# A layer boundary in quarters, a reordered attention tail and an attention without filler products, in a one-core fp32 transformer kernel

## The reference

```python
for i in range(2):                                   # first block
    h = h + 0.5 * rmsnorm(swiglu(rmsnorm(h)))        # sublayers 0 and 3
    m = neighborhood_attention(...) if i == 0 else diff_attention(...)   # 1 and 4
    h = h + rmsnorm(m)
    h = h + 0.5 * rmsnorm(swiglu(rmsnorm(h)))        # 2 and 5
x = h[:, 16:]                                        # second block
x = x + rms_norm(concat(moba_attention(...), mlstm(...)) @ w_out)        # 6
x = x + rms_norm(square(relu(rms_norm(x) @ w_up)) @ w_down)              # 7
```

## Time and profile before

| | |
|---|---|
| time before, median of 3 runs | 1430.26 us (1430.21 to 1435.5) |
| the profiled execution | 1431.02 us, span 1429.2 us |
| PE, PEld busy | 99%, 95% of the span |
| DVE, ACT, POOL busy | 67%, 46%, 3% |
| granted TensorE clock | 1.00 |
| chain that ended last | PE 92%, DVE 4%, ACT 2% |

### The profile page before, as it was taken

The page is one execution under the profiler, slowest core; times in us unless marked ns, Lnnn a source line. Parts: engine busy times, 40 slices in busy tenths (PEclk is TensorE's granted clock), DMA queues, the critical chain, the costliest instruction groups (busy, mean ns, idle before and its releaser), DMA issues.

```text
span 1429.2 us, 26250 instructions
## 1 busy us (share of the span) xinstructions
PE 1415.9 (99%) x10980; PEld 1358.7 (95%) x10980; DVE 950.5 (67%) x1242; ACT 663.5 (46%) x891; POOL 45.0 (3%) x72
## 2 busy tenths in 40 slices
PE   9999999999999999999999999999999999999998
PEld 9999999978999999999999988999999997999887
DVE  6666568565966556866556678776556875787653
ACT  5444436454544334544435357554344455544432
POOL 0000010010000001000001000000001010000000
PEclk9999999999999999999999999999999999999999
DMA  6586765511455576455455640465556540356552
GB/s 220 179 227 189 207 186 172 177 62 53 154 177 176 170 206 211 154 177 177 139 174 159 206 148 2 153 201 185 186 181 200 178 148 31 119 180 212 183 196 98
DMA packets 238911, 234.11 MB, mean 164 GB/s; under 512 B 29791, under 2 KB 233492, under 8 KB 238816
## 3 DMA queue, kind: packets, MB, share of 16 engines
q1 hardware_dynamic: 238024, 232.33, 52.2%
q10 hardware_dynamic: 792, 0.40, 0.1%
HBM read 231.52 MB, written 1.12 MB: 163 GB/s over the span
## 4 chain that ended last, share of the span: by engine, by line
PE 92%; DVE 4%; ACT 2%; issue 1%; DMA 1%; DVEq 0%; SPq 0%; ACTq 0%
PE acc L649 22%; PE acc L648 22%; PE acc L650 22%; PE acc L718 3%; PE aux L888 2%; PE aux L887 2%; PE aux L886 2%; PE acc L724 2%; PE aux L948 1%; PE aux L649 1%; PE aux L650 1%; PE aux L648 1%; PE acc L1161 1%; PE acc L1269 1%; PE aux L1180 1%
## 5 line engine op out<-in xcount | busy, mean ns | idle before, releaser
L648 PE MATMUL acc<-x_hi,w_hi 128*128 128x272 f32 (+1 forms) x1960 | 559.6, 286 | 0.8 <-DVE x_lo L2239 0.6
L649 PE MATMUL acc<-x_lo,w_hi 128*128 128x272 f32 (+1 forms) x1960 | 559.7, 286 | 0.0
L650 PE MATMUL acc<-x_hi,w_lo 128*128 128x272 f32 (+1 forms) x1960 | 557.9, 285 | 0.0
L1880 DVE TENSOR_TENSOR w_lo<-raw,w_hi 128x2048 fp32r<-128x2048 f32 (+2 forms) x224 | 470.3, 2104 | 107.1 <-ACT w_hi L1407 106.7
L1407 ACT ACTIVATE w_hi<-raw 128x2048 fp32r<-128x2048 f32 (+3 forms) x246 | 397.5, 1621 | 156.6 <-DMA raw<-in_ffn_w_down 48.0
L648 PEld LDWEIGHTS acc<-x_hi,w_hi 128*128 128x128 f32 x1960 | 369.4, 188 | 3.6 <-issue 1.7
L649 PEld LDWEIGHTS acc<-x_lo,w_hi 128*128 128x128 f32 x1960 | 368.2, 188 | 0.3 <-issue 0.2
L650 PEld LDWEIGHTS acc<-x_hi,w_lo 128*128 128x128 f32 x1960 | 368.4, 188 | 0.0
L648 PE MATMUL acc<-hid_hi,w_hi 128*128 128x272 f32 (+1 forms) x704 | 201.9, 287 | 0.0
L649 PE MATMUL acc<-hid_lo,w_hi 128*128 128x272 f32 (+1 forms) x704 | 201.6, 286 | 0.0
L650 PE MATMUL acc<-hid_hi,w_lo 128*128 128x272 f32 (+1 forms) x704 | 200.7, 285 | 0.0
(11 more groups left out here) (340 smaller groups left out, 1668.0 us busy)
## 6 DMA issues: line engine op xcount, KB each, us to landing
raw<-in_ffn_w_gate SPq DMA_DIRECT2D x44, 1024.0 KB, 5.3
raw<-in_ffn_w_up SPq DMA_DIRECT2D x44, 1024.0 KB, 5.3
raw<-in_ffn_w_down SPq DMA_DIRECT2D x32, 768.0 KB, 4.5
raw<-in_ffn_w_down SPq DMA_DIRECT2D x32, 640.0 KB, 4.1
raw<-in_w_up SPq DMA_DIRECT2D x16, 1024.0 KB, 5.3
raw<-in_w_down SPq DMA_DIRECT2D x16, 1024.0 KB, 4.8
raw<-in_na_w_qkv SPq DMA_DIRECT2D x12, 1024.0 KB, 5.2
raw<-in_da_w_qkv SPq DMA_DIRECT2D x12, 1024.0 KB, 5.2
```

What stands on the lines that cost most here:

```text
L648: nc.tensor.matmul(o, wh, xh, start=first, stop=False)
L649: nc.tensor.matmul(o, wh, xl, start=False, stop=False)
L650: return nc.tensor.matmul(o, wl, xh, start=False, stop=last)
L1880: nc.vector.tensor_tensor(w_lo[:, slot, w], raw[:, slot, w], w_hi[:, slot, w].bitcast(F32), ALU.subtract)\
```

## The change

Four edits. The panel after the second mixer is split in quarters, as it is after the other sublayers that aren't mixers (`DA` leaves the exceptions; `pieces_before` tells the quarters inside that mixer from those behind it). The calls of `keep_warm` in `mix_attention` go. The tail of `na_attention` has another order, with `blocks_add(1)` ahead of `na_turn(2)`, and without its `keep_warm`. The angles are worked out one panel later.

```diff
-        def pieces_before(k):
-            return 3 * [0, 2, 3, DA, 5].index(k)
+        def pieces_before(k, inside=False):
+            return 3 * [(0, False), (2, False), (3, False), (DA, True), (DA, False), (5, False)].index((k, inside))
...
# shared_chunk (PE), boundary and output_steps (ACT), residual and output_steps (DVE)
-                        in_pieces = n % 2 == 0 and j == 1 and n // 2 - 1 not in (NA, DA, MIX)
+                        in_pieces = n % 2 == 0 and j == 1 and n // 2 - 1 not in (NA, MIX)
...
-                in_pieces = k not in (NA, DA, MIX)
+                in_pieces = k not in (NA, MIX)
...
-                    if local == last - 1 and k in (NA, DA, MIX):
+                    if local == last - 1 and k in (NA, MIX):
...
# mix_attention (PE)
-                        if step % 3 == 1 or step > 11:
-                            keep_warm(aux[:, step % 2, 3 * P:], 2)
...
-                    if step in (1, 2):
-                        keep_warm(aux[:, 3, :], 4)
...
-                    if step > n:
-                        keep_warm(aux[:, 0, :] if step == n + 1 else acc_flat[:, 1, :], 3)
...
# na_attention (PE)
+                na_values(12)
+                na_turned(14)
                 na_turn(0)
                 na_turn(1)
+                na_values(13)
+                na_turned(15)
                 pe.wait_ge(s["logits"], 32)
-                na_turned(14)
-                na_values(12)
-                keep_warm(aux[:, 0, 3 * P:], 3)
-                na_turned(15)
-                na_values(13)
                 keys_turn(1)
                 na_values(14)
                 na_values(15)
+                blocks_add(1)
                 na_turn(2)
                 na_turn(3)
-                blocks_add(1)
...
# mix_part (DVE)
-                if (i, j) == (0, 2):
+                if (i, j) == (0, 3):
                     dve.wait_ge(mix_full, 16 * 7)
```

More of the change, by code:

```diff
@@ L1935, in low_piece @@
                 if piece < 3:
-                    dve.wait_ge(hi_piece, pieces_before(k) + piece + 1)
+                    dve.wait_ge(hi_piece, pieces_before(k, n == 2 * DA + 1) + piece + 1)
                 else:
```

## The result

The change makes the kernel slightly slower: 1435.42 us, median of 20 runs (1431.78 to 1440.08), against 1431.51 for the kernel before, also of 20. The ratio is 1.0026, with a 95% interval of 1.0017 to 1.0036. The forecast was 1426.1 (1423.6 to 1429.3), made from the 1430.26 that stands above as the median of three. The profiled execution took 1434.96 us, span 1432.8. It lost its time in one place, the third mixer's attention, and there to TensorE's clock. In all 20 executions of the changed kernel the mean granted clock is 0.985 to 0.995.

The account below looks back on a forecast made before the run. PE's own order was taken to set the time nearly everywhere. Boundary 0.9, attention 3.0, tail -0.1 and angles 0.3 sum to 4.1 us gained: from 1430.26 to 1426.1 us, range 1423.6 to 1429.3.

Parts of the forecast that it names:

- the third rival: Third mixer's attention: PE idles without filler, clock falls to 1.2 GHz, work takes twice as long, 1434 us; chance 0.08.
- the attention's term: Third mixer's attention: 8.2 us of products on ones go, part becomes waits, 3.0 us gained; bounds 0 and 8.2.
- the wait of unit 14: Third mixer's attention: PE waits some 2.3 us ahead of unit 14's turning, for ACT's exponential (`probs`).
- The attention's mechanism: Third mixer's attention, step by step: first scores to chunk 2 of the output takes 37.5 us instead of 40.6.
- The boundary: After the second mixer: with quarters DVE scales the residual at 910.0 instead of 910.88; 0.9 us gained, bounds 0 and 2.3.
- The first mixer's tail: End of the first mixer's attention: the wait moves to `na_turn(4)`, 0.1 us lost; bounds 1.7 gained, 0.4 lost.
- The angles: Third mixer's projections: panel (1, 1) starts without its 0.3 us wait, 0.3 gained; bounds 0.3 gained, 0.5 lost.
- Panel (1, 2): Third mixer's projections: its `w_lo` ends at 1137.3, PE comes to it at 1137.4, so not late by 0.1 us.

Follow-up runs that it names:

- the version with everything: Changed kernel with picking products padded to 128 rows, eight products on ones in each of two PE waits, second pair of squares earlier: 1426.68 us, ratio 0.9970.
- the boundary alone: Kernel before with the second mixer's boundary in quarters and nothing else: 1431.02 us (0.9983 to 1.0011).
- the few executions at that clock: Changed kernel, picking products padded to 128 rows, eight products in unit 14's wait; three executions at clock 1.000: 1427.15, 1427.27, 1428.72 us; median of all 1431.20.
- the square: Kernel before with the second mixer's boundary in quarters and the second pair of squares ahead of panel (0, 2)'s w_lo: 1431.83 us; 1429.69 at clock 1.000.

## Why the prediction was wrong

**The step that failed** is the judgment on the third rival, "*The clock falls* ... Against: the earlier trace rows", and with it the attention's term, which took the filler as work that PE needn't do. The earlier trace rows come from a boundary between large products of 128 rows, with filler of its own; they say nothing of 40 us of small products. The filler that I removed had all 128 rows and stood among scores of 64 rows and gate products of 4, and I had read it only as time. With it gone the clock was at half for 27 us, and the attention took 44.9 us where 37.5 was forecast. The rival's chance, 0.08, was too small, and its place was wrong: I looked for the fall behind the wait of unit 14, and it came at 1182.9, behind the first wait for `wt`. Its 1434 lies near the measured 1435.4 by luck: it was reckoned from 8 us of the output projection, which ran at 1.00 but for its first microsecond. And 10.3 + 17.1 = 27.4 us at half clock cost 7.5 us (below), where its "every microsecond of work takes two" gives 13.7; in the changed kernel at half clock no wait ahead of unit 14 shows, PE is the late one there, and how the difference divides wasn't measured. The Trainium skill, TensorE: Matmul & The Clock Gate, section Part 1: The HAM clock gate, whose rule I quoted, says that activity releases the throttle; the changed trace agrees in that the clock fell to 0.50 once the filler was gone, but at 1203.4 it fell behind 10.2 us in which PE was shown as busy for 10.03, which the sentence alone doesn't tell.

**The attention's mechanism** was right. In the version with everything the clock is 1.00 throughout, and its PE shows the steps (first scores, the products in the wait of unit 14 and what follows, chunk 2 of the output):
```profile
1176.35 0.49 PE L1020 MATMUL aux<-proj 64*128 64x128 f32 x2
...
1204.89 2.00 PE L949 MATMUL aux<-ones 128*128 128x128 f32 x16
1207.10 0.33 PE L1052 MATMUL aux<-ident,probs 128*128 128x128 f32 x1 [0.20 <-ACT probs L1578]
...
1213.73 0.38 PE L649 MATMUL acc<-x_hi,w_hi 128*128 128x256 f32 x1 [0.64 <-DVE x_lo L2239]
```
It takes 1213.73 - 1176.35 = 37.4 us (forecast 37.5), so 3.2 us return (forecast 3.0); PE has 1207.10 - 1204.89 = 2.2 us to fill ahead of unit 14 (forecast 2.3).

**The boundary** (0.9 forecast): 1.3 at the place itself, 0.6 of it given back at 941, so 0.7 in the changed trace, 0.6 in that of the boundary alone, and none that the times of the boundary alone show. The term was followed from `post_sum` to the first L718 only. The chain of DVE and ACT that feeds the next panels moved by 0.5 us, and it was already as late as PE.

**The first mixer's tail** (0.1 lost): the wait moved as forecast, from 0.29 to 0.88 us, and `evict_rows` started at 338.91 where 338.8 was forecast:
```profile
338.91 0.24 DVE L2339 RECIPROCAL row_recip<-row_sums 128x16 f32<-128x16 f32 x1
```
`na_turn(4)` starts 340.66 - 340.42 = 0.24 us later than before, but PE is 0.28 us later already ahead of the tail (the same turn of a pair starts at 324.80 and at 324.52), so the tail itself loses nothing.

**The angles** (0.3 gained): panel (1, 1) no longer waits, and returns 0.4. Panel (1, 2), which I had safe by 0.1 us, starts 1136.92 - 1136.67 = 0.25 us after the last product instead of 0.12, and its `w_lo` ends just there:
```profile
1130.28 0.23 DVE L2364 CAST angle<-pos_i 128x256 f32<-128x256 int32 x1
...
1134.59 2.28 DVE L1873 TENSOR_TENSOR w_lo<-raw,w_hi 128x2048 fp32r<-128x2048 f32 x1
```
PE's starts keep 0.2 us of the gain.

At clock 1.00 the four terms measure 0.7 + 3.2 + 0.0 + 0.2 = 4.1 us by the traces, and the few executions at that clock (3.75 us, the middle one of three) are near it. That this is the forecast sum is partly luck: two terms came out 0.2 and 0.1 lower, two 0.2 and 0.1 higher. (1430.26 - 4.1 is 1426.2, not the 1426.1 put down; nothing hangs on it.) The low clock took 44.9 - 37.4 = 7.5 us in the attention.

What stays open: whether the waits or the products of few rows weigh more in the first fall (at 1182.9 both precede it); why some executions lose their clock with all the filler in place; and 0.5 of the 1.3 us that the square brought, which its trace doesn't show.

## What to carry to other kernels

Filler in a stretch of small products isn't free time to be taken back: read what the other products there fill, and price the stretch at half clock first. Inside a wait filler cost next to nothing here (37.4 us with sixteen such products, 37.5 forecast without), and a product of a few rows that has to run anyway can be padded with zero rows (0.70 us against 0.69). Where a boundary gets shorter, follow the engines behind it up to the next place where PE meets them; what they were late by before comes back there.

## What the runs showed of the hardware

Products on ones with 4 rows, in the same number and of the same columns as those with 128, didn't hold TensorE's clock: 0.50 for 54 of 61 us, against 1.00 throughout in the profiled execution with 128 rows (five of its twelve executions were at 1.000, and none of the six with 4 rows was above 0.988). PE was shown as busy all the while, so here the busy share didn't tell whether the clock would hold. Zero rows added to four pairs of products raised the mean clock of the executions from between 0.989 and 0.999 to between 0.999 and 1.000, at the same duration of the products. And executions of one kernel differ: ten of 35 of the kernel before ran at a mean clock of 0.996 or 0.997 and took 4 to 5 us longer, while in another series none of 25 did; the 1435.5 among the first three runs of it is of that size. One profile at 1.00 is no proof that the clock holds.
